# Squares of the norms added by GpSimd, and modulation weights in column blocks on partition groups

## The reference

```python
def rms_norm(x, g):
    y = xf * lax.rsqrt(jnp.mean(xf * xf, axis=-1, keepdims=True) + RMS_EPS)
    return (y * g.astype(jnp.float32)).astype(x.dtype)

c_act = jax.nn.silu(c)
mod = c_act @ ada_w[l] + ada_b[l]          # 1024 x 9216 per layer, first block
sh1, sc1, g1, sh2, sc2, g2, sh3, sc3, g3 = jnp.split(mod, N_MOD, axis=-1)
h = modulate(rms_norm(x, norm_ffn1[l]), sh1, sc1)
x = x + 0.5 * g1[:, None, :] * swiglu(h, ffn1_w_in[l], ffn1_w_out[l])
```

## Time and profile before

| | |
|---|---|
| median of 3 runs | 2223.14 us (2218.72 to 2224.87) |
| span of the profiled execution | 2222.6 us |
| PE busy | 2155.5 us, 97% |
| DVE busy | 1674.6 us, 75% |
| ACT busy | 990.5 us, 45% |
| GpSimd busy | 31.1 us, 1% |
| DMA moved | 417.47 MB, 188 GB/s in the mean |

### The profile page before, as it was taken

The page is one execution under the profiler, slowest core; times in us unless marked ns, Lnnn a source line. Parts: engine busy times, 40 slices in busy tenths (PEclk is TensorE's granted clock), DMA queues, the critical chain, the costliest instruction groups (busy, mean ns, idle before and its releaser), DMA issues.

```text
span 2222.6 us, 36384 instructions
## 1 busy us (share of the span) xinstructions
PE 2155.5 (97%) x15539; PEld 1993.2 (90%) x15539; DVE 1674.6 (75%) x2327; ACT 990.5 (45%) x1331; POOL 31.1 (1%) x33
## 2 busy tenths in 40 slices
PE   7999999999999999999999899999999999999998
PEld 7999987999999998799998678888888887889998
DVE  6999877788798877778776774777776568987563
ACT  4534434534443443443344664422222348764442
POOL 0000000000000000000000000000000001110000
PEclk9999999999999999999999999999999999999999
DMA  9999744798789864467774102254465232133662
GB/s 322 317 330 309 248 133 150 242 316 298 264 284 305 302 202 153 142 196 248 236 228 142 36 4 74 80 186 155 156 221 189 76 114 69 48 122 127 223 191 76
DMA packets 338631, 417.47 MB, mean 188 GB/s; under 512 B 9274, under 2 KB 263208, under 8 KB 338472
## 3 DMA queue, kind: packets, MB, share of 16 engines
q1 hardware_dynamic: 335360, 411.84, 56.2%
q10 hardware_dynamic: 3112, 3.33, 0.5%
HBM read 414.09 MB, written 1.05 MB: 187 GB/s over the span
## 4 chain that ended last, share of the span: by engine, by line
PE 46%; DVE 7%; ACT 3%; issue 2%; POOL 0%; DVEq 0%; ACTq 0%
PE pb L623 45%; ACT wh L1461 1%; DVE wl L2100 1%; DVE T L2108 1%; PE pb L1289 1%; DVE ACC L2108 1%; DVE SM L2694 1%; DVE RS L2192 0%; DVE Hl L2108 0%; DVE L_y L2108 0%; ACT A_P L1935 0%; DVE L_y L2100 0%; ACT L_y L1462 0%; DVE L_y L2815 0%; DVE L_u L2108 0%
## 5 line engine op out<-in xcount | busy, mean ns | idle before, releaser
L623 PE MATMUL pb<-Hh,wh 128*128 128x256 f32 (+1 forms) x2624 | 795.5, 304 | 13.8 <-DVE wl L2100 5.4
L623 PE MATMUL pb<-Hl,wh 128*128 128x256 f32 (+1 forms) x2624 | 779.3, 297 | 0.0
L623 PE MATMUL pb<-Hh,wl 128*128 128x256 f32 (+1 forms) x2624 | 774.7, 297 | 0.0
L2100 DVE TENSOR_TENSOR wl<-raw,wh 128x2048 fp32r<-128x2048 f32 (+3 forms) x271 | 600.9, 2222 | 179.9 <-ACT wh L1461 179.1
L1461 ACT ACTIVATE wh<-raw 128x2048 fp32r<-128x2048 f32 (+3 forms) x271 | 502.2, 1855 | 357.6 <-PE pb L623 259.0
L623 PEld LDWEIGHTS pb<-Hh,wh 128*128 128x128 f32 x2624 | 504.6, 192 | 33.5 <-issue 9.6
L623 PEld LDWEIGHTS pb<-Hl,wh 128*128 128x128 f32 x2624 | 504.9, 192 | 15.3 <-issue 2.2
L623 PEld LDWEIGHTS pb<-Hh,wl 128*128 128x128 f32 x2624 | 501.9, 192 | 12.8
L623 PE MATMUL pb<-Bh,wh 128*128 128x256 f32 (+1 forms) x1376 | 420.1, 305 | 7.1 <-DVE Y L2100 2.5
L623 PE MATMUL pb<-Bl,wh 128*128 128x256 f32 (+1 forms) x1376 | 413.5, 300 | 0.0
L623 PE MATMUL pb<-Bh,wl 128*128 128x256 f32 (+1 forms) x1376 | 413.4, 300 | 0.0
(11 more groups left out here) (256 smaller groups left out, 2113.9 us busy)
## 6 DMA issues: line engine op xcount, KB each, us to landing
raw<-in_ada_w_dram SPq DMA_DIRECT2D x126, 1024.0 KB, 5.5
raw<-in_ffn_w_in_dram SPq DMA_DIRECT2D x88, 1024.0 KB, 6.7
raw<-in_mlp_w_dram SPq DMA_DIRECT2D x64, 1024.0 KB, 5.3
raw<-in_ffn_w_out_dram SPq DMA_DIRECT2D x32, 1024.0 KB, 6.5
raw<-in_mix_w_in_dram SPq DMA_DIRECT2D x22, 1024.0 KB, 5.7
raw<-in_ffn_w_out_dram SPq DMA_DIRECT2D x16, 768.0 KB, 4.6
raw<-in_attn_w_qkv_dram SPq DMA_DIRECT2D x12, 1024.0 KB, 6.2
raw<-in_lru_w_in_dram SPq DMA_DIRECT2D x10, 1024.0 KB, 5.1
```

Of the source, the lines that this page charges most:

```text
L623: return e.matmul(o, l, r, start=st, stop=sp, skip_group_check=True)
L2100: return e.tensor_tensor(o, a, b, f)
```

## The change

Two things are changed.

**Modulation pieces.** All pieces but the six of the first two segments hold q = 2 or 4 column blocks of 512 columns. Block j lies on its own group of 128/q partitions, so a piece has 4 x 128/q rows of q x 512 columns. A piece stays 1 MB and is issued as q transfers of 64 or 32 partitions. A group has 2q pieces for 1024 rows; DVE makes 8q passes over it into one accumulator, and `flush` multiplies by q columns with ones on one group's partitions each, so four products give 4q columns. q is 4 where two neighbouring segments are due together, else 2. silu(c) is laid out for the groups in a new tile `CW` (six more transposes on PE, two copies on DVE, one Silu on ACT, at the start). The order of the stream stays, position by position.

**Norms.** GpSimd adds squares. In an ordinary norm it adds those of tiles 1 to 5 onto tile 0's, and PE makes three products: of that total, of tile 6 and of tile 7. In the context's norm and the four norms of each seam it adds all, and PE makes one product. As one slot (4) holds the total, the squares go round three others. The first norm, that of the recurrence's output and the last one keep their form.

```diff
@@ constants: block columns of ones
+K_BLK = {1: K_ONE, 2: 385, 4: 387}
+    for q in (2, 4):
+        k[p, K_BLK[q] + p // (128 // q)] = 1.0
+FOLD_SLOT = (4, 5, 6, 7, 5, 6, 7, 5)
+FOLDED = 6
@@ build: the pieces of the modulation
+        if seg in ((0, 0, 0), (0, 0, 1)):
...
+                adas.append(Piece(b, l, s, i // 2, 1, i % 2, vecs, due[seg], [src]))
+            continue
+        q = 2
+        if order and order[0] == (b, l, s + 1, *only) and due[order[0]] == due[seg]:
+            order.pop(0)
+            q = 4
+        for i in range(2 * q):
+            rows = w[512 // q * i:512 // q * (i + 1)]
+            adas.append(Piece(b, l, s, 0, q, i, vecs, due[seg], [rows[:, s * 1024 + 512 * j:s * 1024 + 512 * j + 512] for j in range(q)]))
@@ the column of silu(c) that a pass multiplies by
+        def c_col(q, v, kk):
+            k, a = divmod(kk, q)
+            if q == 1:
+                return CV[:, 8 * v + k:8 * v + k + 1]
+            c = (0 if q == 4 else 96) + 24 * a + 8 * v + k
+            return CW[:, c:c + 1]
@@ SyncE: the issue of a piece
-                parts = [(0, 4, 0, 512, u[4])] if kind == "a" else u[3]
+                if kind == "a":
+                    n = 128 // u.q
+                    for j, src in enumerate(u.parts):
+                        e.dma_start(view[n * j:n * j + n, :, :], src.rearrange("(k p) n -> p k n", p=n)).then_inc(sems[f"raw{p % RAW}"], 16)
+                    continue
@@ TensorE: flush
+                blocks = KM[:, K_BLK[u.q]:K_BLK[u.q] + u.q]
                 for h in range(4):
-                    ins = mm(PB[7][:, c0 + h:c0 + h + 1], ACC[:, a, h * 128:h * 128 + 128], KM[:, K_ONE:K_ONE + 1], True, True)
+                    ins = mm(PB[7][:, c0 + h:c0 + h + 4 * u.q - 3:4], ACC[:, a, h * 128:h * 128 + 128], blocks, True, True)
@@ TensorE: an ordinary norm's sums (new class Folded)
+                    for i, kt in enumerate((0, *range(FOLDED, 8))):
+                        if i:
+                            E.wait_ge("sq", q0 + kt + 1)
+                        else:
+                            E.wait_ge("fold", f0 + FOLDED - 1)
+                        E.mark(mm(self.p[:, 0:self.n], ONES, T[:, FOLD_SLOT[kt], 0:self.n], i == 0, kt == 7), "fold.read")
@@ TensorE: the context's norm in the first feed-forward block
-                            for kt in range(8):
-                                E.wait_ge("sq", E.up("sq"))
-                                mm(csum.p[:, 0:256], ONES, c_slot(kt), kt == 0, kt == 7).then_inc(sems["sq.read"], 1)
+                            E.wait_ge("fold", E.up("fold", 7))
+                            E.mark(mm(csum.p[:, 0:256], ONES, c_slot(0), True, True), "fold.read")
@@ TensorE: a seam's sums (class Seam; of_x, second_x, of_c and second_c each call it once)
+                def total(self, p, n, seg):
+                    E.wait_ge("fold", self.folded[n])
+                    E.mark(mm(p[:, SEG[seg]], ONES, T[:, 4, SEG[seg]], True, True), "fold.read")
@@ ScalarE: a square of an ordinary norm (new function folded_square)
+                if kt > 3:
+                    E.wait_ge("fold", E.n["fold"] - (FOLDED - 1) + kt - 3)
+                z = T[:, FOLD_SLOT[kt], :]
+                act(z[:, 0:n], src, ACT.Square).then_inc(sems["sq"], 1)
@@ VectorE: a pass over a piece (take)
-                            col = 8 * v + 4 * (i % 2) + k
-                            c = CV[:, col:col + 1]
-                            if k == 0 and i % 2 == 0:
+                            c = c_col(u.q, v, 4 * u.i + k)
+                            if k == 0 and u.i == 0:
@@ GpSimd
+            def add_squares(dst, src, k):
+                E.wait_ge("sq", k)
+                E.wait_ge("fold", E.n["fold"])
+                E.mark(e.tensor_tensor(dst, dst, src, ALU.add), "fold")
+            def folded(n):
+                q0 = E.n["sq"]
+                E.up("sq", 8)
+                for kt in range(1, FOLDED):
+                    add_squares(T[:, 4, 0:n], T[:, FOLD_SLOT[kt], 0:n], q0 + kt + 1)
+            def seam_folded(c, first=1):
...
+                for kt in range(first, 8):
+                    add_squares(T[:, 4, c], T[:, FOLD_SLOT[kt], c], q0 + kt + 1)
```

More of the change, by code:

```diff
@@ L239, in build @@
     adas, direct = [], []
-    for seg in sorted(due, key=lambda s: (due[s], s)):
+    order = sorted(due, key=lambda s: (due[s], s))
+    while order:
+        seg = order.pop(0)
         b, l, s, *only = seg
@@ L264, in build @@
     room = np.concatenate([[0.0], np.cumsum(at_unit)])
-    cost = np.cumsum([len(a[2]) for a in adas])
+    cost = np.cumsum([len(a.vecs) for a in adas])
     ends = {}
     for a, c in zip(adas, cost):
-        ends[a[3]] = c
+        ends[a.due] = c
     stream, ai, budget, sent = [], 0, 0.0, 0
@@ L285, in build @@
     for p, (kind, u) in enumerate(stream):
-        seen[p % RAW] += 16 * (len(u[3]) if kind == "w" else 1)
+        seen[p % RAW] += 16 * len(u[3] if kind == "w" else u.parts)
         LAND.append(seen[p % RAW])
@@ L908, in ffn @@
                     if c == last:
-                        sums = Sums(512 if l and seg else 256)
+                        sums = Folded(512 if l and seg else 256)
                     for m in range(4):
@@ L913, in ffn @@
                         fm("fo", "fo", hid_at(b), 256, hid_need, said="x", by=2)
-                        if c == last and m:
-                            sums.add(2 * m)
                 return sums
@@ L1105, in _ @@
                 full(e.transpose(fill("su")[:, 0:n], VR[tile][0:n, :], KM[0:n, K_ID:K_ID + n]), "su")
+            E.wait_ge("dve.step", 3)
+            pw = fill("su")
+            for a in range(6):
+                z = VW4[:, 128 * a:128 * a + 128] if a < 4 else VW2[:, 128 * a - 512:128 * a - 384]
+                ins = e.transpose(pw[:, 24 * a:24 * a + 24], z, KM[0:24, K_ID:K_ID + 24])
+            full(ins, "su")
             direct_cols(1)
@@ L1196, in mlp @@
                         mods(*late)
[L1197 removed]
+                        seam = Seam(sums, SUMS2[1], (7, 7, 7, 7), 32)
                         us = [weights("m2")]
@@ L1218, in _ @@
             sums.add()
-            SQUARES["first"] = E.n["sq"]
+            SQUARES["first"] = E.n["fold.read"]
             cx_rest(between)
@@ L1570, in ffn @@
                     late_loads()
+                    act(CW[:, :], full("su")[:, 0:144], ACT.Silu).then_inc(sems["su.read"], 1)
                 if seg or l:
```

245 lines of the change are left out of this document (138 added, 107 removed).

## The result

The changed kernel took 2388.53 us in the median of 4 runs (2384.15 to 2407.96), the kernel before 2224.01. The ratio is 1.0757, with a 95% interval of 1.0729 to 1.0786: slower by 165 us, where 22 us less were forecast and the range ended at 2250.

A forecast was written before the change was run, and what follows sets the result against it. PE, busy 97% of a 2222.6 us span, was taken as the bound. The terms 1 + 20 - 6 - 4 - 15 - 8 - 8.6 - 0.9 = -21.5 us gave 2202 us, range 2164 to 2250.

The forecast's parts named there:

- the term that decides: How long a modulation piece in parts takes to land: 4.3 us, giving +20 us in 46–235 and -4 in 410–800.
- its other bytes, 84.5: In 46–235, the DMA time of everything but the modulation pieces, 164 - 79.5 = 84.5 us, taken as unchanged.
- 29t - 104.5: Change of 46–235 if DMA becomes the bound, t being one piece's landing time; for 410–800 it is 45t - 201.3.
- the bound of 5.48: Upper bound in us for landing a modulation piece in parts: half the way into memory, parts following one another.
- rival (b): Slower parts make DMA the bound, first feed-forward block, from about 4.6 us a piece: 2235 at 4.8, 2285 at 5.48; chance 0.26.
- The choice within the bounds: For a modulation piece in parts, 4.3 us was taken between 2.74 and 5.48.
- PE's saving: Over the kernel, 48 flushes and 89 square products go: 41.0 + 32.8 + 7.7 = 81.5 us off PE.
- The start: Six more transposes on PE, two copies on DVE and one Silu on ACT: +1 us.
- The seams: Between attention and MLP and between layers, most of 24.0 us saved on PE becomes waiting; a third kept: -8 us.
- 235–410 and 800–1325: Stretches with DMA room, where PE's saving less 1 us each is won: -6 and -15 us.
- The GB/s of 46–235: Sign to check in the profile after: the DMA rate there falls from 321 to about 290.
- (a): Parts land like whole pieces, 2.74 us: -4 in 46–235, -13 in 410–800, in all -54.5 us, 2169 us; chance 0.30.

The follow-up runs named there:

- transfers_alone: No compute, only weight transfers on SP's queue in several forms: a modulation piece took 2.71 us whole, 4.63 in neighbouring parts, 2.74 strided.
- transfers_shallow: No compute, modulation and feed-forward pieces in turn with 4, 3 or 2 in flight: a pair in neighbouring parts took 8.0, 8.0 and 7.8 us.
- norms_only: The changed kernel with the modulation pieces and 75 flushes of the kernel before, only the norms' squares on GpSimd: 2237.53 us, ratio 1.0063.
- whole_pieces: The changed kernel with each modulation piece fetched in one transfer over 128 partitions, from the places of the kernel before: 2215.78 us, ratio 0.9960.

## Why the prediction was wrong

- **The step that failed** is "the term that decides", in two ways. First, the price of a piece in parts was 4.3 us; transfers alone show 4.63, and the packets of the changed kernel add to 4.9 for a piece (141.3 us / 29, 219.4 / 45). Second, and more, the working put it on the 29 and 45 modulation pieces alone and left the feed-forward pieces at their 2.9 us ("its other bytes, 84.5"). In the kernel they slowed with them, to 4 or 5 us, and a pair took 10.0 us in 46–235 (median) where the sum had 7.2. At t = 4.63 the prediction's own lines give +30 and +7 us, where 84 and 92 were measured. Turned round, 29t - 104.5 = 84 and 45t - 201.3 = 92 both give t = 6.5 us. That is no longer the time of a modulation piece, as it carries the others' delay. It is above the bound of 5.48, so even rival (b)'s far end, 2285, fell short: the bound held for the transfer and not for what stands beside it in the same queue.
- **Rival (b)** was the right mechanism, in the right place, from the right point (4.64 against a measured 4.63 alone). It was given 0.26. The row that spoke for it was the share of 0.95 in 46–235. The price of the other pieces is in none of the rivals.
- **The choice within the bounds** was made "somewhat above the middle", on the idea that several parts in flight, with whole pieces between them, cover part of a doubling. The runs show no such cover: a piece took 4.63 us with four pieces in flight (transfers_alone) and 4.66 with two (transfers_shallow), and the parts' packets took as long with whole pieces between them (150 to 157 ns) as without (152 to 154).
- **PE's saving**: 48 flushes and 89 products went, as counted. Its worth was overestimated where nothing seemed to stand in the way: with whole pieces the flushes brought 22 us of 41 (norms_only to whole_pieces), 13 with the norms of before (9 to 18).
- **The start**, +1: measured +7.7, nearly all of which came back by placing the six transposes later.
- **The seams**, -8: measured +11.6 with the pieces, +11.5 without (norms_only). The mechanism, an addition that lands after wl, was right; its size was not. Only the last additions' delay was priced, and that was near (the addition ends 0.6 us after wl, the next takes 0.7). Not priced were the DVE operations that the additions hold up (0.42 to 0.94 us each), nor that PE stands still at a product in which all eight are gathered.
- **235–410 and 800–1325**: -21 forecast, -2.7 measured. With whole pieces it was still only -6, and in norms_only 1200–1325 alone lost 4.2, at a mean clock of 0.96. What holds these stretches was not found.
- The GB/s of 46–235 were to fall to about 290; they fell to 222. The check that was to tell (a) from (b) did so at a glance.

## What to carry to other kernels

A transfer that writes part of the partitions should write partitions spread over all of them (every q-th), not a block: the same bytes, transfers and sums cost 171 us less here. When one kind of piece gets slower in a shared queue, price the pieces behind it as well, from the rate of the whole stretch. And of the PE time taken out here, in a kernel whose other engines are near it, a third to a half remained; look at what the engine waits for next, and at its clock, before counting the rest.

## What the runs showed of the hardware

- Parts on 32 or 64 neighbouring partitions ran at 226 and 227 GB/s, on every second or fourth at 388 and 382, whole at 384, and the share of busy time was nearly the same in all (1.05 to 1.07). A 2 KB packet took 152 to 154 ns in neighbouring parts, 88 to 89 in the others.
- With neighbouring parts in the queue the 16 shares of a whole piece can fall out of step (5 to 8 us from first to last in the mean, 0.3 and 0.7 in the two stretches that stayed in step), and then the whole pieces' 1 KB packets slow from 56 to 72 ns, the parts' own packets not. This was seen with and without compute; what begins it is open.
- With six small transposes on 24 partitions ahead of the first flushes the granted clock fell to 0.5 at 28 to 30 us for 17 to 21 us (six kernels); with the transposes 8 us later it fell at 34 to 36 us for 7 us, as before the change (four kernels).
- A GpSimd addition of 128x256 took 0.72 to 0.74 us alone. Begun while DVE subtracted for wl (two operands in SBUF) it ended 0.58 to 0.60 us after that instruction, 17 times of 17. DVE's addition of 128x256, begun beside one of GpSimd's, took 0.94 in place of 0.42.
